# The causal mask of the prompt's window and selected scores, added on TensorE instead of VectorE

## The chip, the cores and the metric

The kernel runs on one core of one Trainium2 chip. The metric is the device time of one execution, in microseconds, of the whole program; lower is better. The times shown are the median of several executions; the profile is one further execution.

## The reference, cut to what matters

One inference step of a two-layer decoder: layer 0 is a causal convolution module, layer 1 is native sparse attention; each has a squared-ReLU MLP and a gated embedding behind it. A prompt of 512 tokens and 64 sample tokens (8 sequences of 8) share the weights. The part that the change touches is the attention of the prompt in layer 1, for its selected-block and its window branch:

```
lw = einsum('bqgrd,bkgd->bqgrk', q_rot, kw) * scale
pw = softmax(where(wmask, lw, NEG), axis=-1)       # wmask: key position <= query position
o_win = einsum('bqgrk,bkgd->bqgrd', pw, vw)
ls, ps, o_sel: the same with the selected branch's keys and values
out = gates0 * o_cmp + gates1 * o_sel + gates2 * o_win
```

With 512 tokens, 16 blocks to choose and 8 there, and a window of 512, both branches see every key up to the query's own position. So a tile of 128 queries needs all key tiles before it in full, and a triangle of the key tile on the diagonal. NEG is -1e30.

## The kernel before, in words

The program is written out by hand for each engine; the engines meet at counted semaphores (`x.then_inc(s, 1)`, `engine.wait_ge(s, n)`). Every engine runs its own instructions strictly in the order written.

Most of the span is dense layers: weights are split into a high and a low part in the type float32r, and three matmuls (lines 611 to 613) with 288 moving columns each make one product. These are the rest of the program, and the change does not touch them.

The prompt's attention is a software-pipelined loop over 64 pairs `PAIRS[i] = (c, r, n)`: chunk c (two heads, 8 of them), query tile n (0 to 3, 128 queries each), branch r (selected or window). A pair has two heads e, which lie on partitions 0 to 63 and 64 to 127. The pair with query tile n has (n+1)*128 keys, so that the work of a pair goes from 1 to 4 units and a chunk has 8 pairs. For each pair:

- TensorE, `p_scores(i)` (lines 944 to 952): two float32 matmuls, one per head, on 64 rows of the array each, into PSUM banks 2*(i%2) and the next. It waits until the exponentials of pair i-2 have been read out of these banks, and signals `p_mm`.
- VectorE, `p_top(i)` (lines 1676 to 1686): adds the 128x128 table `causal` (0 or -1e30) to the diagonal key tile of both heads in PSUM (line 1683), waits for its own write (`chain`), and takes the negated row maximum (line 1685), which signals `p_max`.
- ScalarE, `p_exps(i)` (line 1308): two exponentials with the maximum as bias, which also sum the rows.
- VectorE, `p_sums` (line 1693): reciprocal of the sums. GpSimd (line 586): multiplies the probabilities by the reciprocal and the gate.
- TensorE, `p_transpose(i-3)` (line 961): n+1 transposes for each head. ScalarE (line 1317, head 0) and VectorE (line 1700, head 1) copy them out of PSUM; the transposes of head e wait until the previous pair's copy of e is done.
- TensorE, `p_out(i-4)` (line 978): 2*(n+1) matmuls of 64 weight columns on the two column halves of the array, and line 971 once for a chunk.

In iteration i TensorE issues `p_scores(i)`, `p_transpose(i-3)`, `p_out(i-4)`; VectorE issues `p_top(i)`, `p_sums(i-1)`, `p_move(i-3)`; ScalarE issues `p_move(i-3)`, `p_exps(i)` and, now and then, the copy of a finished chunk (line 1324). Ahead of the loop TensorE waits for `t_fin` (the last sample's heads, VectorE line 1661) and ScalarE for `t_mm` (the transposes of line 901). Behind the loop comes the dense stage "out": ScalarE and VectorE split the attention's result (lines 1032 and 1371), GpSimd splits the weights (line 532) after its last scaling.

`tab("ident")` and `tab("causal")` are 128x128 float32 tables in SBUF. `hb_byte` is the place of a buffer that is free in this stage; its first 16384 bytes per partition hold `pc_t` and `pt_p`.

Of the kernel before, what the change touches and what calls it, by code (L numbers as in the profile page):

```python
# [16 lines left out]
F32R = mybir.dt.float32r  # L17
I32 = mybir.dt.int32
ACT = mybir.ActivationFunctionType
AX = mybir.AxisListType  # L20

P = 128
D = 1024
SEQ = 512
# [160 lines left out]
def program(nc, ext, out):  # L185
    from contextlib import ExitStack
    with ExitStack() as ctx:
        def sb(name, shape, dt=F32):
            return ctx.enter_context(nc.sbuf_tensor(name, shape, dt))

        def sem(name):
            return ctx.enter_context(nc.semaphore(name))
# [3 lines left out]
        def at_byte(name, shape, byte, dt=F32):  # L196
            return nc.alloc_sbuf_tensor_at(name, shape, dt, offset=byte)
# [19 lines left out]
        hb_byte = arena[0]  # L217
# [24 lines left out]
        q_rot = big[:, at:at + C * T].rearrange("p (c t) -> p c t", t=T); at += C * T  # L242
        kv_cmp = big[:, at:at + 4 * T].rearrange("p (c t) -> p c t", t=T); at += 4 * T
        k_rot = big[:, at:at + 4 * T].rearrange("p (c t) -> p c t", t=T); at += 4 * T
# [40 lines left out]
        rec_p = kvc_flat[:, 2160:2168]  # L285
        k_cmp_p = sb("k_cmp_p", [P, 2, 2, NCP])
        w2 = sb("w2", [P, 2, HD])
        c_vec = sb("c_vec", [P, 2])
        gate_s = sb("gate_s", [P, NB, 3])
        pages = sb("pages", [1, NB * PAGES], I32)  # L290
# [3 lines left out]
        ps = ctx.enter_context(nc.psum_tensor("ps", [P, 8, 512], F32))  # L294
# [36 lines left out]
        def tab(name):  # L331
            a, b = CON[name]
            return con[:, a:b]
# [70 lines left out]
        pt_out = [sem("pt_out0"), sem("pt_out1")]  # L404
        po_mm = sem("po_mm")
        ot_out = sem("ot_out")

        block = ctx.enter_context(nc.Block())

# [181 lines left out]
        def _(pe):  # L591
# [96 lines left out]
            for n, (i, m, j) in enumerate(DIAGONALS):  # L688
                t = FIRST["taps"] + i
                first, end = j == TAP_TILES[i][1], j == TAPS - 1  # L690
                if first:
# [4 lines left out]
                                 stop=end).then_inc(tile_done if end else diag_used, 1)  # L696
# [3 lines left out]
            for i, m in enumerate([None] + LATE):  # L700
# [3 lines left out]
                for a in range(2):  # L704
                    last = nc.tensor.matmul(STAT[:, a, :], tab("mean"), src[:, a * HT:(a + 1) * HT],
                                            start=i == 0, stop=i == len(LATE))
# [21 lines left out]
            for a in range(2):  # L728
                for k in range(C):
                    for w, h in ((wg_hi, ha), (wg_lo, ha), (wg_hi, hb)):  # L730
                        last = nc.tensor.matmul(slot(t)[0:48, a, :], w[:, 48 * k:48 * k + 48], chunk(h, k, a * HT, HT),
                                                start=k == 0 and (w, h) == (wg_hi, ha), stop=k == C - 1 and h is hb)
# [3 lines left out]
            for part in range(2):  # L736
# [3 lines left out]
                for i in range(TT):  # L740
# [3 lines left out]
                    for k in range(C):  # L744
                        nc.tensor.matmul(to, chunk(ha, k, i * P, P), wh[:, 256 * k:256 * k + 256], start=k == 0, stop=False)
                        nc.tensor.matmul(to, chunk(ha, k, i * P, P), wl[:, 256 * k:256 * k + 256], start=False, stop=False)
                        last = nc.tensor.matmul(to, chunk(hb, k, i * P, P), wh[:, 256 * k:256 * k + 256], start=False,
                                                stop=k == C - 1)
# [5 lines left out]
            for i in range(TT):  # L754
                rows = P if i < PT else NS
                last = nc.tensor.transpose(ps[0:rows, 2 * (t % 3), 48 * i:48 * i + 48], gates_f[:, i * P:i * P + rows],
                                           tab("ident")[0:48, 0:48])
# [4 lines left out]
            lo, _ = PAR["pe"]  # L762
            for v in range(2):
                for j in range(16):
                    last = nc.tensor.matmul(ps[0:1, 7, P * v:P * (v + 1)], par[:, lo + 16 * v + j:lo + 16 * v + j + 1],
                                            w1[:, v, j, :], start=j == 0, stop=j == 15)
            last.then_inc(c_mm, 1)
            pe.wait_ge(pairs_in, 16 * 4)
            for v in range(2):
                for j in range(16):  # L770
                    last = nc.tensor.matmul(ps[:, 6, 128 * v:128 * v + 124].rearrange("p (g c) -> p g c", g=KV),  # L771
                                            w1[:, v, j, :], kv_pairs[:, v, :, 2 * j:2 * j + 16 * (NCP - 2) + 1:16],
                                            start=j == 0, stop=j == 15)
                last.then_inc(phid_mm, 1)
            pe.wait_ge(c_there, 1)
            for v in range(2):
                last = nc.tensor.transpose(ps[:, 7, 256 + v:257 + v], c_row[:, P * v:P * (v + 1)], tab("ident")[0:1, 0:1])
# [6 lines left out]
            for g in range(2):  # L784
                for k in range(4):
                    last = nc.tensor.matmul(ps[32 * k:32 * k + 32, 7, 64 + 64 * g:128 + 64 * g],
                                            hid_p[:, 1, k % 2, g, :], w2[:, 1, :], start=True, stop=True)
# [24 lines left out]
            for u in range(2 * NB):  # L812
                b, v = u // 2, u % 2
                i = B_OF["cmp_pages", b]
# [3 lines left out]
                for half in range(2):  # L818
                    for j in range(8):
                        rhs = block_at(i, 0, BLK).rearrange("p (a n) -> p a n", a=PAGES)[:, :, 256 * v + 32 * j:256 * v + 32 * j + 32]  # L820
                        last = nc.tensor.matmul(ps[:, 2 * (u % 3) + half, 0:256], w1[:, v, 8 * half + j, :], rhs,  # L821
                                                start=j == 0, stop=j == 7)
# [9 lines left out]
            for b in range(NB):  # L832
                for g in range(2):
                    last = nc.tensor.matmul(ps[64 * g:64 * g + 64, 4, 64 * b:64 * b + 64],
                                            qbd[:, b, g, :, :].rearrange("p e m -> p (e m)"), k_cmp_s[:, b, g, :],
                                            start=True, stop=True)
            last.then_inc(sc_mm, 1)
            for n in range(PT):
                for c in range(C):
                    last = nc.tensor.matmul(ps[:, n, 2 * NCP * c:2 * NCP * (c + 1)], q[:, c, n * P:(n + 1) * P],  # L840
                                            k_cmp_p[:, c // 4, :, :].rearrange("p e c -> p (e c)"), start=True, stop=True)
                last.then_inc(sc_mm, 1)
                if n == 1:
# [5 lines left out]
                    for j in range(4):  # L849
                        last = nc.tensor.transpose(ps[:, 6, 128 * j:128 * j + 128], pc_s[:, 128 * j:128 * j + 128], tab("ident"))  # L850
                    last.then_inc(ct_mm, 1)
            for n in range(PT):
# [5 lines left out]
                for j in range(4):  # L858
                    last = nc.tensor.transpose(ps[:, 4 + n % 2, 128 * j:128 * j + 128], pc[n][:, 128 * j:128 * j + 128],
                                               tab("ident"))  # L860
# [48 lines left out]
            for b in range(NB):  # L909
                if b + 1 < NB:  # L910
                    scores_s(b + 1)
                i = B_OF["sel_pages", b]
# [5 lines left out]
                for k, tiles in enumerate(([0, 128, 256, 384], [512, 640, 768, 896], [1088, 1216, 1344, 1472], [1024, 1600])):  # L918
                    to = t_slot(t_group(b, k))
                    w = P if k < 3 else NS  # L920
                    for j, at in enumerate(tiles):
                        last = nc.tensor.transpose(to[0:w, 128 * j:128 * j + 128], pp[:, at:at + w], tab("ident"))
# [10 lines left out]
                for j in range(4):  # L933
                    nc.tensor.matmul(ps[:, 6, 256:512], pt_s[:, 1024 + 128 * j:1152 + 128 * j],
                                     win[:, 2 + j // 2, 256 * (j % 2):256 * (j % 2) + 256],
                                     start=j == 0, stop=False)
# [7 lines left out]
            def p_scores(i):  # L944
                c, r, n = PAIRS[i]
                if i >= 2:
                    pe.wait_ge(p_exp, i - 1)
                for e in range(2):
                    part = slice(64 * e, 64 * e + 64)
                    last = nc.tensor.matmul(ps[:, 2 * (i % 2) + e, 0:(n + 1) * P], q_rot[part, c, n * P:(n + 1) * P],  # L950
                                            k_rot[part, 2 * r + c // 4, 0:(n + 1) * P], start=True, stop=True)
                last.then_inc(p_mm, 1)

            def p_transpose(i):
# [26 lines left out]
                last.then_inc(po_mm, 1)  # L981

            pe.wait_ge(t_fin, NB)
            N = len(PAIRS)
            for i in range(N + 4):
                if i < N:
# [17 lines left out]
        def _(act):  # L1004
# [140 lines left out]
            for m in range(C):  # L1145
                p = tile("pw1", 2 * m)
# [177 lines left out]
                nc.scalar.activation(attn_t[:, c, 0:SEQ], ps[:, 6 + c % 2, :], ACT.Copy).then_inc(ot_out, 1)  # L1324

            act.wait_ge(t_mm, 5 * NB)
            N = len(PAIRS)
            for i in range(N + 3):
                if i >= 3:
# [21 lines left out]
        def _(dve):  # L1351
# [173 lines left out]
            def chain(ins):  # L1525

                after(step(ins))
# [148 lines left out]
            def p_top(i):  # L1676
                n = PAIRS[i][2]
                dve.wait_ge(p_mm, i + 1)
                if i >= 4:
                    dve.wait_ge(p_exp, i - 3)  # L1680
                lo, col = 2 * (i % 2), 2 * (i % 4)
                s = ps[:, lo:lo + 2, n * P:(n + 1) * P]
                chain(nc.vector.tensor_tensor(s, s, tab("causal").rearrange("p (o k) -> p o k", o=1).to_broadcast((P, 2, P)),
                                              ALU.add))
                nc.vector.tensor_reduce(nmax_p[:, col:col + 2].rearrange("p (e o) -> p e o", o=1), ps[:, lo:lo + 2, 0:(n + 1) * P],
                                        AX.X, ALU.max, negate=True).then_inc(p_max, 1)

# [191 lines left out]
```

## Time and profile before

| what | value |
|---|---|
| median of 3 runs | 1984.52 us (1984.49 to 1991.64) |
| profiled execution, its own time | 1990.01 us |
| its span, first to last instruction | 1987.9 us |
| mean granted TensorE clock | 0.956 of 2.4 GHz |
| TensorE busy | 1836.5 us (92%) |
| VectorE, ScalarE, GpSimd busy | 775.7, 644.1, 601.3 us |
| the loop over the 64 pairs | about 1254.8 to 1411.5 us of the span |

"Busy" is the union of the instructions' durations on an engine; matmuls overlap each other, so the time that a matmul costs in a stream is the distance between starts, not its duration. A float32 matmul shows as two records, a float32r matmul and a transpose as one. "PEclk" is the granted TensorE clock as a share of 2.4 GHz: 1.00 or 0.50, or a mean of both over a stretch.

### The profile page before, as it was taken

Reading aid. Unit: us, or ns where it says so; the run is one execution under the profiler, and the core shown is the slowest. Engines: PE = TensorE matmul, PEld = TensorE weight load, DVE = VectorE, ACT = ScalarE, POOL = GpSimd, SP = SyncE. Lnnn points to the kernel's source line nnn. Section 1 sums busy time; section 2 is a strip of 40 time slices with the busy share of each in tenths; the row PEclk is TensorE's granted clock in tenths of the full one; section 3 lists DMA queues with packets and bytes.
Section 4 is the critical chain, followed back from the end, with each engine's and each line's share of the span. In section 5 each row is a group of like instructions: output and inputs, shape, how many; then the busy total and the mean of one; then the engine's idle time right before and its main releaser. Section 6 shows DMA issues by size and latency. Waiting matters only on the chain.

```text
span 1987.9 us, 30013 instructions
## 1 busy us (share of the span) xinstructions
PE 1836.5 (92%) x12689; PEld 1648.1 (83%) x12689; DVE 775.7 (39%) x1130; ACT 644.1 (32%) x1042; POOL 601.3 (30%) x292
## 2 busy tenths in 40 slices
PE   5999679999999998999899698899878999999998
PEld 5974669999999988999788455466768999999988
DVE  5979535021212245152000633577435121222242
ACT  4243534232222233422111232477433232222231
POOL 3653113333333312332100000355412333333322
PEclk9999779999999999999899799899989999999999
DMA  6253111222222211134542667100111222122211
GB/s 207 85 58 29 43 43 64 85 86 85 85 85 79 79 72 69 64 97 115 165 138 85 222 214 242 43 2 1 55 64 64 85 80 91 65 87 84 85 64 69
DMA packets 62326, 175.86 MB, mean 88 GB/s; under 512 B 22754, under 2 KB 23666, under 8 KB 48690
## 3 DMA queue, kind: packets, MB, share of 16 engines
q1 hardware_dynamic: 59346, 164.66, 26.3%
q0 software_dynamic: 2720, 8.42, 1.2%
q8 instruction: 100, 1.64, 0.3%
q10 hardware_dynamic: 128, 0.88, 0.3%
q14 instruction: 32, 0.26, 0.0%
HBM read 155.55 MB, written 15.41 MB: 86 GB/s over the span
## 4 chain that ended last, share of the span: by engine, by line
PE 83%; DVE 9%; ACT 3%; issue 2%; DMA 1%; SPq 1%; POOL 1%; ACTq 0%; DVEq 0%; POOLq 0%
PE ps L611 20%; PE ps L613 20%; PE ps L612 20%; PE ps L821 6%; PE ps L950 3%; PE ps L961 2%; PE ps L978 2%; DVE ps L1472 2%; PE ps L648 2%; DVE hb L1371 1%; PE ps L931 1%; PE ps L678 1%; PE ps L877 1%; DVE sq_sum L1384 1%; PE ps L771 1%
## 5 line engine op out<-in xcount | busy, mean ns | idle before, releaser
L532 POOL TENSOR_TENSOR w_lo<-w_raw,w_hi 128x2048 fp32r<-128x2048 f32 x98 | 452.9, 4622 | 896.6 <-ACT w_hi L1014 896.6
L611 PE MATMUL ps<-ha,w_hi 128*128 128x288 f32 x1920 | 573.3, 299 | 26.3 <-DVE hb L1371 24.8
L612 PE MATMUL ps<-hb,w_hi 128*128 128x288 f32 x1920 | 571.3, 298 | 0.0
L613 PE MATMUL ps<-ha,w_lo 128*128 128x288 f32 x1920 | 571.1, 297 | 0.0
L611 PEld LDWEIGHTS ps<-ha,w_hi 128*128 128x128 f32 x1920 | 366.0, 191 | 29.9 <-issue 17.6
L612 PEld LDWEIGHTS ps<-hb,w_hi 128*128 128x128 f32 x1920 | 366.1, 191 | 0.0
L613 PEld LDWEIGHTS ps<-ha,w_lo 128*128 128x128 f32 x1920 | 366.0, 191 | 0.0
L611 PE MATMUL ps<-hid_hi,w_hi 128*128 128x288 f32 x1024 | 301.8, 295 | 0.0
L612 PE MATMUL ps<-hid_lo,w_hi 128*128 128x288 f32 x1024 | 301.6, 295 | 0.0
L613 PE MATMUL ps<-hid_hi,w_lo 128*128 128x288 f32 x1024 | 301.6, 295 | 0.0
L1014 ACT ACTIVATE w_hi<-w_raw 128x2048 fp32r<-128x2048 f32 x98 | 186.9, 1907 | 171.4 <-PE ps L613 165.5
L1402 DVE TENSOR_TENSOR sq<-sq 128x576 f32<-128x576 f32 x64 | 94.8, 1482 | 314.1 <-ACT sq L1096 314.1
L613 PEld LDWEIGHTS ps<-hid_hi,w_lo 128*128 128x128 f32 x1024 | 192.3, 188 | 0.0
L612 PEld LDWEIGHTS ps<-hid_lo,w_hi 128*128 128x128 f32 x1024 | 192.1, 188 | 0.0
L611 PEld LDWEIGHTS ps<-hid_hi,w_hi 128*128 128x128 f32 x1024 | 192.0, 188 | 0.0
L1412 DVE TENSOR_TENSOR mix<-ps,mix 128x576 f32<-128x576 f32 x48 | 36.4, 758 | 237.4 <-PE ps L613 237.2
L821 PE MATMUL ps<-ring,w 128*128 128x256 f32 x512 | 115.7, 385 | 0.0
L821 PEld LDWEIGHTS ps<-ring,w 128*128 128x128 f32 x512 | 96.9, 192 | 16.1 <-issue 2.9
L586 POOL TENSOR_SCALAR big<-big,gates 128x128 f32<-128x128 f32 (+3 forms) x128 | 77.0, 611 | 101.5 <-DVE big L1693 100.8
L1472 DVE SCALAR_TENSOR_TENSOR ps<-big,par,ps 128x512 f32<-128x512 f32 x156 | 103.5, 749 | 0.0
L1096 ACT ACTIVATE sq<-ps 128x576 f32<-128x576 f32 x64 | 41.6, 650 | 165.8 <-PE ps L613 165.8
L580 POOL DMA_DIRECT2D out_win<-attn_t x8 | 5.8, 722 | 257.4 <-DMA attn_t<-in_win 257.4
(238 smaller groups left out, 2170.0 us busy)
## 6 DMA issues: line engine op xcount, KB each, us to landing
w_raw<-in_w SPq DMA_DIRECT2D x98, 1024.0 KB, 4.8
ring<-in_cmp_pages SPq DMA_DIRECT2D x64, 256.0 KB, 3.0
ring<-in_sel_pages SPq DMA_DIRECT2D x64, 256.0 KB, 3.2
attn_t<-in_win SPq DMA_DIRECT2D x16, 512.0 KB, 5.4
out_win<-attn_t POOLq DMA_DIRECT2D x8, 1024.0 KB, 5.3
x<-in_x SPq DMA_DIRECT2D x4, 576.0 KB, 5.5
out_y<-x SPq DMA_DIRECT2D x8, 288.0 KB, 2.1
w_raw<-in_ple SPq DMA_DIRECT2D x2, 1024.0 KB, 4.7
```

The source lines that it names most:

```text
L532: nc.gpsimd.tensor_tensor(w_lo[j % 2][:, :], w_raw[:, k, :], w_hi[j % 2][:, :].bitcast(F32), ALU.subtract).then_inc(w_ready, 1)
L586: nc.gpsimd.tensor_scalar(rows, rows, rec_p[:, 2 * (i % 4) + e:2 * (i % 4) + e + 1], gates[:, n, gate:gate + 1], ALU.mult, ALU.mult).then_ ...
L611: nc.tensor.matmul(to, wh, chunk(hi, k, a * HT, HT), start=k == 0, stop=False)
L612: nc.tensor.matmul(to, wh, chunk(lo, k, a * HT, HT), start=False, stop=False)
L613: return nc.tensor.matmul(to, wl, chunk(hi, k, a * HT, HT), start=False, stop=k == C - 1)
L648: last = nc.tensor.matmul(slot(t)[:, a, :], w[:, k, m * P:(m + 1) * P], ple_in[:, k, a * HT:(a + 1) * HT], start=k == 0, stop=k == 1)
L821: last = nc.tensor.matmul(ps[:, 2 * (u % 3) + half, 0:256], w1[:, v, 8 * half + j, :], rhs, start=j == 0, stop=j == 7)
L950: last = nc.tensor.matmul(ps[:, 2 * (i % 2) + e, 0:(n + 1) * P], q_rot[part, c, n * P:(n + 1) * P], k_rot[part, 2 * r + c // 4, 0:(n + 1) ...
L1014: nc.scalar.activation(w_hi[j % 2][:, :], w_raw[:, k, :], ACT.Copy).then_inc(w_hi_ready, 1)
L1096: nc.scalar.activation(halves(raw(name, m)), p, ACT.Relu).then_inc(act_freed, 1)
L1402: nc.vector.tensor_tensor(r, r, r, ALU.mult).then_inc(raw_ready, 1)
L1472: on_way.append(step(nc.vector.scalar_tensor_tensor(to, e, w, sums, ALU.mult, ALU.add)))
```

## The change

TensorE gets, in every pair, two more matmuls behind the two score matmuls: the identity as weights and the causal table as 128 moving columns, both in float32r, accumulated onto the diagonal key tile of each head. VectorE's addition goes, and the wait on its own write with it. The two tables are copied once, by ScalarE, into a float32r buffer `mask_r` behind `pt_p`, ahead of the loop; TensorE waits for both copies before its first pair.

```diff
+        mask_r = at_byte("mask_r", [P, 2, P], hb_byte + 32 * SEQ, F32R)
...
+        mask_ready = sem("mask_ready")
...
                 for e in range(2):
                     part = slice(64 * e, 64 * e + 64)
-                    last = nc.tensor.matmul(ps[:, 2 * (i % 2) + e, 0:(n + 1) * P], q_rot[part, c, n * P:(n + 1) * P],
-                                            k_rot[part, 2 * r + c // 4, 0:(n + 1) * P], start=True, stop=True)
+                    nc.tensor.matmul(ps[:, 2 * (i % 2) + e, 0:(n + 1) * P], q_rot[part, c, n * P:(n + 1) * P],
+                                     k_rot[part, 2 * r + c // 4, 0:(n + 1) * P], start=True, stop=False)
+                for e in range(2):
+                    last = nc.tensor.matmul(ps[:, 2 * (i % 2) + e, n * P:(n + 1) * P], mask_r[:, 0, :], mask_r[:, 1, :],
+                                            start=False, stop=True)
                 last.then_inc(p_mm, 1)
...
             pe.wait_ge(t_fin, NB)
+            pe.wait_ge(mask_ready, 2)
...
             act.wait_ge(t_mm, 5 * NB)
+            nc.scalar.activation(mask_r[:, 0, :], tab("ident"), ACT.Copy).then_inc(mask_ready, 1)
+            nc.scalar.activation(mask_r[:, 1, :], tab("causal"), ACT.Copy).then_inc(mask_ready, 1)
...
                 lo, col = 2 * (i % 2), 2 * (i % 4)
-                s = ps[:, lo:lo + 2, n * P:(n + 1) * P]
-                chain(nc.vector.tensor_tensor(s, s, tab("causal").rearrange("p (o k) -> p o k", o=1).to_broadcast((P, 2, P)),
-                                              ALU.add))
                 nc.vector.tensor_reduce(nmax_p[:, col:col + 2].rearrange("p (e o) -> p e o", o=1), ps[:, lo:lo + 2, 0:(n + 1) * P],
                                         AX.X, ALU.max, negate=True).then_inc(p_max, 1)
```

## Rows read from the trace of the kernel before

**Rows 1.** The profile page: TensorE's busy time, and the chain that ended last.

```profile
PE 1836.5 (92%) x12689; PEld 1648.1 (83%) x12689; DVE 775.7 (39%) x1130; ACT 644.1 (32%) x1042; POOL 601.3 (30%) x292
PE 83%; DVE 9%; ACT 3%; issue 2%; DMA 1%; SPq 1%; POOL 1%; ACTq 0%; DVEq 0%; POOLq 0%
```

**Rows 2.** Busy time by stretch: length, then each engine's busy us (instructions), PEclk.

```profile
1275.00:1402.00 127.00, 125.95 (x1062) 76.64 (x1064) 94.97 (x221) 88.47 (x284) 66.05 (x110) 1.00 0.01 2
1285.49:1303.92 18.43, 18.31 (x156) 11.12 (x155) 13.86 (x33) 12.47 (x42) 9.62 (x16) 1.00 0.01 2
1322.35:1340.93 18.58, 18.35 (x155) 11.12 (x155) 13.90 (x33) 14.05 (x43) 9.62 (x16) 1.00 0.00 1
1254.80:1275.00 20.20, 17.85 (x78) 8.35 (x78) 11.13 (x26) 9.04 (x33) 6.58 (x12) 0.59 0.18 77
```

**Rows 3.** Chain of waits inside one chunk: start us, us, what, xrecords.

```profile
1290.95 1.06 PE ps L950 x4
1292.01 0.81 PE ps L961 x6
1292.82 0.59 PE ps L978 x8
1293.40 0.42 PE ps L950 x4
1293.83 0.48 PE ps L961 x3
1294.31 0.12 issue
1294.42 0.52 PE ps L961 x3
...
1296.17 1.02 PE ps L961 x8
```

**Rows 4.** Groups by line, loop only: line, engine, operation, shapes, count, busy, mean ns.

```profile
L1683 DVE TENSOR_TENSOR ps<-ps,con 128x256 f32<-128x256 f32 x64 | 27.6, 431 | 37.3 <-PE ps L950 36.8
```

**Rows 5.** VectorE in order of time beside the gap at 1294.31: start us, us.

```profile
1292.06 0.43 DVE L1683 TENSOR_TENSOR ps<-ps,con 128x256 f32<-128x256 f32 x1
1292.53 1.23 DVE L1685 TENSOR_REDUCE big<-ps 128x2 f32<-128x1024 f32 x1
1293.74 0.54 DVE L1700 COPY pt_p<-ps 128x384 f32<-128x384 f32 x1
```

**Rows 6.** Chain of waits in two float32r stages: 256 and 288 moving columns.

```profile
908.01 0.12 PE ps L747
1424.34 0.13 PE ps L613
```

**Rows 7.** Weight loads, whole run: float32r, float32, transposes; mean ns behind busy us.

```profile
L612 PEld LDWEIGHTS ps<-hb,w_hi 128*128 128x128 f32 x1920 | 366.1, 191 | 0.0
L931 PEld LDWEIGHTS ps<-ring,sq 128*128 128x128 f32 x128 | 23.7, 190 | 4.4 <-ACT sq L1296 1.0
L961 PEld LDWEIGHTS ps<-con,big 128*128 128x128 f32 x320 | 34.3, 143 | 33.6 <-issue 17.2 <-POOL big L586 14.7
```

**Rows 8.** Float32 matmuls of 64 columns, 128x128 weights: TensorE in order of time.

```profile
1110.77 3.54 PE L840 MATMUL ps<-k_cmp_p,big 128*128 128x64 f32 x29
```

**Rows 9.** Chain of waits ahead of the loop and into its first pair.

```profile
1247.91 0.65 PE ps L931 x3
...
1249.18 1.92 PE ps L934 x8
...
1254.42 0.37 DVE attn_t L1661 x2
...
1254.84 0.82 PE ps L950 x4
...
1255.68 0.45 DVE ps L1683
```

**Rows 10.** ScalarE's copies of an SBUF table of 128x128: duration min/median/max ns.

```profile
L1142 ACT ACTIVATE diag<-con,par x74: 386/401/403, 117.6 to 177.8; 128x128 f32<-128x128 f32 x74
```

**Rows 11.** GpSimd in order of time at the loop's end.

```profile
1404.78 3.13 POOL L586 TENSOR_SCALAR big<-big,gates 128x512 f32<-128x512 f32 x4 [0.93 <-DVE big L1693]
1407.88 9.01 POOL L532 TENSOR_TENSOR w_lo<-w_raw,w_hi 128x2048 fp32r<-128x2048 f32 x2
```

**Rows 12.** Chain of waits from the loop's end into the stage "out".

```profile
1404.68 0.47 DVE pt_p L1700
1405.15 0.14 issue
1405.28 0.52 PE ps L961 x3
...
1412.86 4.66 DVE ha L1371
```

## Prediction

> **What bounds the kernel now.** I read the page's busy line and its chain first: TensorE is busy 92% of the span and holds 83% of the chain [rows 1]. That is an average over stages, so the next view is the busy time by stretch, on the loop that the change touches. From 1275 to 1402 us TensorE is busy 125.95 of 127.00 us at the full clock, VectorE 94.97, ScalarE 88.47, GpSimd 66.05 [rows 2]. A chunk of 8 pairs takes 18.43 us, of which TensorE is busy 18.31 and VectorE 13.86. Busy on TensorE can hide gaps, since the ends of matmuls are modelled. So the third view is the chain of waits inside a chunk, where each piece runs from start to start [rows 3]. The pieces follow each other with nothing between, and their lengths are a plain function of the work: transposes take 0.81 us for 6 and 1.02 us for 8, that is 0.107 us each and 0.16 to 0.17 us for entering and leaving the group. The scores take 1.06 us for 512 columns and 0.42 us for 128, 0.213 us for each 128 columns. A stage that waited on another engine would not keep such lengths. It has one exception in a chunk: 6 transposes that take 0.48 + 0.12 + 0.52 = 1.12 us instead of 0.81, about 0.3 us lost at 1294.31 [rows 3]. What TensorE waits for there is VectorE's copy of head 1, which starts at 1293.74 and takes 0.54 us, behind an addition of 0.43 us and a reduction of 1.23 us [rows 5].
>
> So in steady state the loop is TensorE's, by a margin of a quarter over VectorE, and VectorE costs it about 0.3 us in a chunk. The addition that goes is 64 instructions of 0.431 us, 27.6 us in sum [rows 4], and nearly all of that lies beside TensorE's work.
>
> **What the change removes.** VectorE loses 0.43 us and the hand-over to its own next instruction (0.45 us from start to the next piece in the chain [rows 9]; 0.47 us from start to start [rows 5]) in each pair. Beside TensorE's work this is worth nothing. It is worth something in three places. (a) The gap of about 0.3 us in a chunk: VectorE's copy now comes earlier against TensorE's scores and TensorE arrives later, so the gap closes; 7 chunks from the first such gap behind 1275 make -2.1 us, and shorter gaps in some chunks (18.58 us instead of 18.43 in one, [rows 2]) some -0.2: -2.3 us. (b) The first pairs, where scores, maximum and exponentials hang on each other: part of (d) below. (c) The end: GpSimd scales the last two pairs from 1404.78 for 3.13 us and then splits two weight blocks until 1416.89 [rows 11]; VectorE's 4.66 us part that opens the next stage lies beside that and ends at 1417.52 [rows 12]. The scaling hangs on the reciprocal behind the last pair's reduction. That reduction comes 0.47 us earlier by the missing addition and 0.22 us later by the mask matmuls: -0.25 us. The closed wait of 0.14 us at 1405.15 is inside that.
>
> **What it adds, in each pair.** Two matmuls of 128x128 weights and 128 moving columns. No row of before shows a float32r matmul under 256 columns. Float32r matmuls take 0.12 us from start to start with 256 columns and 0.13 us with 288 [rows 6]: 256 and 288 columns at 2.4 GHz are 0.107 and 0.120 us, so each has some 13 ns on top, and 128 columns would need 0.053 + 0.013 = 0.067 us if nothing else bound them. The weights do: float32 matmuls of 64 columns, whose two records need only 0.053 us of columns each, run at 0.11 to 0.12 us for each record (3.54 us for 29, [rows 8]); and a float32r weight load lasts as long as a float32 one, 191 ns against 190 ns, where that of a transpose lasts 143 ns [rows 7]. So I take 0.11 us for the load of each mask matmul. The two heads' weights are the same, but each matmul carries its own load.
>
> In sequence: the scores leave the 64-row form of the array and the next group enters the 128-row form, before and after the change; before, the transposes pay for that, now the first mask matmul does, with a longer exposed load. Eight float32 matmuls that enter the same way take 1.92 us [rows 9], 0.19 us over 8 steps of 0.216 us (0.65 us for 3), where transposes pay 0.16 to 0.17: the exposed load costs 0.03 to 0.05 us more. Then comes one step of 0.11 us (the second load), and the second mask matmul itself 0.067 us, with the transposes' shorter load under it. First load and step, second matmul: 0.05 + 0.11 + 0.067 = 0.22 to 0.23 us in each pair; I take 0.22. Bounds from rows: 0.13 us if the loads cost nothing (two times 0.067); 0.43 to 0.47 us if 128 columns of float32r take what 128 columns of the float32 scores take, 0.213 us [rows 3]; and 0.37 us if the way from a float32r matmul to a transpose costs an entering and leaving of its own, 0.15 us more.
>
> The Trainium skill speaks to this in "TensorE: Matmul & The Clock Gate", section "LDWEIGHTS": a load takes as many ns as its columns divided by 1.2, 107 ns for 128; the row of 64-column matmuls agrees (0.11 to 0.12 us). The same page, section "Weight-path perf modes", has a rule by which it comes out cheaper: a fast weight load is on when there are 128 weights and the type is not FP32, and float32r might count as such. By the traces a float32r load lasts 191 ns and a float32 load 190 ns, so the trace speaks against it; it is a rival below. "TensorEngine Tiling", section "Key Properties", says that changing the tiling mode drains the engine; the trace shows such a cost at every group (0.16 to 0.19 us), and whether a float32r matmul ahead of a transpose is a change of mode no row shows.
>
> (d) **The first 8 pairs.** This stretch runs at a granted clock of 0.59 in the mean [rows 2], 0.50 in most of it. Pairs 0 to 3 hang on the exponentials; there the score's signal comes later by the masks and an additional change of form (about 0.6 us at half clock) and VectorE saves 0.47: +0.13 us on each of two hops. From pair 4 TensorE binds: two pairs at half clock, 2 x 0.44, and two at full clock, 2 x 0.22. Sum +1.6 us. Bounds 0 and +4.
>
> (e) **Ahead of the loop.** ScalarE's two copies wait for the same transposes as VectorE's line 1661, and TensorE now waits for both. A copy of such a table takes 401 ns [rows 10]; two in a row, overlapped by 0.1 us, end 0.7 us after 1254.42 instead of VectorE's 0.37 us [rows 9]: +0.3 us. Queued behind that wait on TensorE is only the loop itself. The copies read and write SBUF and cover nothing else; ScalarE has nothing to do until the first maximum at 1256.6. Bounds 0.2 and 0.5.
>
> **The sum.** Behind the eighth pair, 55 pairs carry their 0.22 us to the last score: 55 x 0.22 = 12.1. With (a) -2.3, (c) -0.25, (d) +1.6, (e) +0.3: +11.5 us. The rest of the program follows shifted. The profiled execution was 1990.01 us, its span 1987.9; it lies 5.5 us over the median 1984.52, which one of the three runs (1991.64) does too, so such a difference is between executions and I carry the sum over to the median: 1984.5 + 11.5 = 1996.0 us, +0.58%. With 0.19 to 0.26 us for a pair and the bounds of (d) and (e) this case runs from 1992 to 2001.
>
> **The rivals.**
> 1. Four passes: float32r with only 128 columns costs what float32 costs. For it: all float32r rows have 256 columns or more, so nothing shows that the low price holds below. Against: at 256 and 288 the time is columns over the clock plus a constant. A pair pays 0.47 us, 0.25 more: 57 x 0.25 = +14: 2010 us.
> 2. A change of form between mask and transposes: +0.15 us a pair, 57 x 0.15 = +8.5: 2004.5 us. The change from 64 to 128 rows shows the price; between two 128-row forms no row shows it.
> 3. Cheap masks, on the other side (not slower): the weight loads of float32r are fast or lie under the drain of the scores. A pair pays 0.13 us: 55 x 0.13 = 7.2, (d) halves to 0.8, the rest as above: +5.7, 1990.2 us, within what can be told from no change. It turns into a gain at a price for a pair under about 0.04 us, which no row comes near. The rule on fast loads named above would be its mechanism.
> 4. VectorE sets the loop after all, and TensorE's gapless look is the model's. Then 64 x 0.47 = 30 us would go and some 1970 us be left. Against it: VectorE's 75% of the stretch, and group lengths that follow the work alone.
>
> **How the numbers follow.** Forecast 0.55, rival 1 0.2, rival 2 0.1, rival 3 0.12, rival 4 0.03. Times of this kernel can be told from no change at about 0.5%, 9.9 us. The forecast's own range straddles that a little (1994.4), and so do single executions 7 us apart: three quarters of it count as slower. Slower: 0.41 + 0.2 + 0.08 = 0.69; faster: rival 4, 0.03; the rest, 0.28, within 0.5%. The range takes in rival 3 and rival 1: 1989.5 to 2011.
>
> **What would show it.** Right: the added matmuls start about 0.16 and then 0.11 us apart, and the transposes less than 0.1 us behind the second; a chunk takes 18.4 + 8 x 0.22 - 0.3 = 19.9 us instead of 18.43; the piece of three and three transposes has no gap; VectorE's busy time in the loop falls by 27.6 us while TensorE stays over 98%. Wrong: steps of 0.2 us or two records for a mask matmul (rival 1); 0.15 us or more between the second mask and the transposes (rival 2); a chunk at or under 18.4 us (rival 4); new waits on `p_exp` or `p_scaled` on TensorE, which I cost at nothing, because every pair gives the other engines more time than before.

## The result, and the profile after

| | median of runs | lowest to highest | profiled execution | its span | its granted clock |
|---|---|---|---|---|---|
| before | 1986.94 us (5 runs) | 1984.49 to 1991.64 | 1990.01 us | 1987.9 us | 0.956 |
| after | 2002.59 us (5 runs) | 1997.77 to 2006.75 | 1997.77 us | 1995.8 us | 0.96 |

The ratio after/before is 1.0074, 95% interval 1.0055 to 1.0092: the change makes the kernel slower by 0.55 to 0.92%, 11 to 18 us. I had forecast 1996.0 us with a range of 1989.5 to 2011 and a chance of 0.69 for slower. The kernel before came out at 1986.94 us here, and at 1988.5 to 1989.3 us in three comparisons with 23 to 29 runs each below. My base of 1984.5 us rested on three runs and was low by 2 to 5 us.

The profile page of the kernel after, its busy line: TensorE has 11.6 us more and 128 records more, VectorE 27.2 us and 64 instructions less than in [rows 1].

```profile
PE 1848.1 (93%) x12817; PEld 1664.0 (83%) x12817; DVE 748.5 (38%) x1066; ACT 644.8 (32%) x1044; POOL 600.8 (30%) x292
```

Busy time by stretch of the kernel after, columns as in [rows 2]: the stretch of the loop and one chunk in it.

```profile
1275.00:1402.00 127.00, 127.00 (x1080) 82.59 (x1077) 66.84 (x153) 81.61 (x260) 59.70 (x101) 1.00 0.01 2
1280.32:1300.39 20.07, 20.07 (x172) 13.09 (x171) 10.58 (x25) 12.44 (x42) 9.57 (x16) 1.00 0.01 2
```

A chunk takes 20.07 us where it took 18.43 [rows 2], and in it TensorE has no idle time at all, while VectorE's busy time falls from 13.86 to 10.58 us. A chunk's length is read from the chain of waits, as the distance between two starts of the piece of 1.05 us that comes once in a chunk (line 971 before, line 976 after).

The chain of waits inside that chunk, kernel after, beside [rows 3]. Its lines 952, 955, 966 and 983 are the scores, the mask matmuls, the transposes and `p_out`:

```profile
1286.27 1.06 PE ps L952 x4
1287.33 0.37 PE ps L955 x2
1287.70 0.68 PE ps L966 x6
1288.38 0.59 PE ps L983 x8
1288.97 0.42 PE ps L952 x4
1289.39 0.37 PE ps L955 x2
1289.76 0.68 PE ps L966 x6
...
1292.04 0.90 PE ps L966 x8
```

Three things can be read here. The scores take what they took (1.06 and 0.42 us). The two mask matmuls (L955) are a piece of 0.37 us, and the transposes behind them are shorter by 0.12 to 0.13 us (0.68 for 6 against 0.81, 0.90 for 8 against 1.02), because the mask now pays for entering the group: 0.37 - 0.125 = 0.245 us a pair, net. And the six transposes that broke into 0.48 + 0.12 + 0.52 us in [rows 3] are one piece.

### The profile page after: what moved, and what is told of

It is laid out like the page before. It is cut to its first block, busy times and chain, and to the rows that moved or that the text cites. A ratio compares the mean times of both kernels' runs of the same rounds, so it can differ in the third digit from the quotient of the medians.

```text
span 1995.8 us, 30207 instructions
## 1 busy us (share of the span) xinstructions
PE 1848.1 (93%) x12817; PEld 1664.0 (83%) x12817; DVE 748.5 (38%) x1066; ACT 644.8 (32%) x1044; POOL 600.8 (30%) x292
## 4 chain that ended last, share of the span: by engine, by line
PE 84%; DVE 8%; ACT 3%; issue 1%; DMA 1%; POOL 1%; SPq 1%; ACTq 0%; DVEq 0%; POOLq 0%
PE ps L613 20%; PE ps L615 20%; PE ps L614 20%; PE ps L823 6%; PE ps L952 2%; PE ps L983 2%; DVE ps L1480 2%; PE ps L966 2%; PE ps L650 2%; PE ps L933 1%; PE ps L955 1%; DVE hb L1379 1%; PE ps L680 1%; PE ps L879 1%; DVE sq_sum L1392 1%
## 5 line engine op out<-in xcount | busy, mean ns | idle before, releaser
L613 PE MATMUL ps<-ha,w_hi 128*128 128x288 f32 x1920 | 573.2, 299 | 24.9 <-DVE hb L1379 23.9
```

What stands on the lines that cost most here:

```text
L613: nc.tensor.matmul(to, wh, chunk(hi, k, a * HT, HT), start=k == 0, stop=False)
```

## The experiments

Of each run the ratio to the kernel before, measured beside it, is given, and the length of a steady chunk, in which the clock is full. In the kernels with mask matmuls and in no_mask the steady chunks repeat to 0.01 us, far finer than the times; in the kernel before, four of six take 18.43 us and two 18.58. (chunk - 18.12) / 8 is the price of a pair's mask, where 18.12 us is the chunk without any mask (no_mask). Line numbers in the lines shown are those of each run's own kernel, and shift by one or two.

**before_again: how fine is the comparison?** No edit.

> The kernel before, unchanged, as a second profile. Its steady chunk (8 pairs) must again take 18.43 us. Open is the first chunk: it took 20.1 us before, with 17.1 us at the half clock, and 17.1 us in the changed kernel, with 6.8 us at the half clock. If the shorter stretch at the half clock is chance (it falls differently from one execution to the next), this run may show a first chunk unlike 20.1 us, or the changed kernel's later profiles will show other values than 17.1. If the change itself shortens it (more work on TensorE), this run shows 20 us again and every kernel with mask matmuls about 17.

1.0014, interval 1.0001 to 1.0028; chunk 18.43 us. The first chunk, from the first score of pair 0 to that of pair 8, takes 18.96 us where it took 20.08, with 13.7 us at half clock instead of 17.1: it differs between executions of one program. The same kernel against itself reads 0.14% off, with an interval that leaves out 1, so nothing under 0.3% is read from a ratio here; the chunks must carry it.

**no_mask: the floor.** The mask is left out.

```diff
-                s = ps[:, lo:lo + 2, n * P:(n + 1) * P]
-                chain(nc.vector.tensor_tensor(s, s, tab("causal")...to_broadcast((P, 2, P)), ALU.add))
```

> The kernel before with the addition of the mask left out altogether (neither engine adds it; the outputs of the prompt are then not causal). Theory (TensorE sets the loop, VectorE costs it one gap of 0.3 us in a chunk): a steady chunk takes 18.15 us instead of 18.43, the total is some 3 us under before, which timing alone can hardly tell. Rival (VectorE's in-order chain sets the loop and TensorE only looks gapless): 8 x 0.47 = 3.8 us less in a chunk, 30 us less in all.

0.9983, 0.9969 to 0.9997. Two starts of the once-a-chunk piece:

```profile
1302.97 1.05 PE ps L971 x2
1321.09 1.05 PE ps L971 x2
```

18.12 us a chunk: taking 64 x 0.43 us from VectorE is worth 0.31 us a chunk. From the first score to the first matmul of the next stage, this trace is 3.9 us shorter than before_again's, which also has 13.7 us at half clock at the loop's start: 0.2% of the time, within the ratio's interval of 0.03 to 0.31%. This is about all that the change could ever have won. Rival 4 (VectorE sets the loop, -1.5%) falls.

**both: VectorE's addition kept beside the mask matmuls.**

```diff
+                s = ps[:, lo:lo + 2, n * P:(n + 1) * P]
+                chain(nc.vector.tensor_tensor(s, s, tab("causal")...to_broadcast((P, 2, P)), ALU.add))
```

> The mask matmuls of the changed kernel with VectorE's addition kept beside them (the mask is added twice). Theory: TensorE pays 0.245 us a pair whether VectorE is relieved or not; a steady chunk takes 18.15 + 8 x 0.245 = 20.1 us plus whatever VectorE's addition still costs it, 0 to 0.3 us: 20.1 to 20.4. Total as the changed kernel, at most 3 us more. Rival (the relief of VectorE is worth much and offsets a larger cost of the masks): a chunk of 22 us or more.

1.0078, 1.0061 to 1.0095. Once-a-chunk starts, and the one group of transposes in a chunk that is longer than 0.68 us:

```profile
1291.95 1.05 PE ps L976 x2
...
1301.39 0.86 PE ps L966 x6
...
1312.21 1.05 PE ps L976 x2
```

20.25 to 20.26 us, 0.18 more than with the masks alone: the addition costs TensorE 0.18 us a chunk even here. So the slowdown is the matmuls' own (18.43 to 20.25 with VectorE's work as it was), and VectorE's relief gives little of it back.

**four_masks: each mask matmul twice.**

```diff
-                for e in range(2):
+                for k in range(4):
+                    e = k // 2
...
-                                            start=False, stop=True)
+                                            start=False, stop=k % 2 == 1)
```

> Each head's mask matmul is issued twice (the mask is added twice), so four in a pair. Theory (a mask matmul costs its weight load, about 0.11 us, whatever waits there are): a chunk takes 20.07 + 16 x 0.11 = 21.8 us and the total is 64 x 0.22 = 14 us over the changed kernel. Rival (most of the cost is paid once, for the change of form or a later signal to VectorE, and the masks themselves are 0.067 us each): 20.07 + 16 x 0.067 = 21.1 us, +8.6 us in all.

1.0159, 1.014 to 1.0178. The masks' piece, and two once-a-chunk starts:

```profile
1295.29 1.05 PE ps L977 x2
...
1302.74 0.59 PE ps L956 x4
...
1317.14 1.05 PE ps L977 x2
```

21.85 us, 1.78 more than after for 16 more matmuls: 0.111 us each.

**one_mask: the mask of head 1 left out.**

```diff
-                                     ..., start=True, stop=False)
-                for e in range(2):
+                                     ..., start=True, stop=e == 1)
+                for e in range(1):
```

> As the changed kernel with the mask matmul of head 0 alone (head 1 of each chunk is left without its mask). It parts the price of a pair, 0.245 us, into the first and the second mask matmul. By four masks in a pair each further one costs 0.111 us: a chunk of 20.07 - 8 x 0.111 = 19.2 us and 0.134 us for the first. If the first pays for the change of form alone and the rest is free (rival), 19.9 to 20.0 us.

1.0013, 0.9998 to 1.0028. The mask's piece, and the once-a-chunk starts:

```profile
1300.66 0.26 PE ps L955
1301.17 1.05 PE ps L976 x2
...
1320.34 1.05 PE ps L976 x2
```

19.17 us: the first mask costs (19.17 - 18.12) / 8 = 0.131 us and the second (20.07 - 19.17) / 8 = 0.112 us, the same as the third and fourth. Each mask is a step of 0.11 us, and the first has 0.02 us on top.

**half_cols: 64 moving columns instead of 128.** The mask is left out of the first 64 keys of the diagonal tile.

```diff
-                    last = nc.tensor.matmul(ps[:, 2 * (i % 2) + e, n * P:(n + 1) * P], mask_r[:, 0, :], mask_r[:, 1, :],
+                    last = nc.tensor.matmul(ps[:, 2 * (i % 2) + e, n * P + 64:(n + 1) * P], mask_r[:, 0, :], mask_r[:, 1, 64:P],
```

> As the changed kernel, but each mask matmul has 64 moving columns instead of 128 (the mask is left out of the first 64 keys of the diagonal tile). It asks what the 0.111 us of a float32r mask matmul is: the load of 128 weight columns, or 128 moving columns. Theory (the load): a chunk stays at 20.0 to 20.07 us. Rival (the columns, at 0.067 us for 128 or twice that): 16 x 0.027 to 16 x 0.053 us less, 19.2 to 19.65 us.

1.007, 1.0041 to 1.0098. Two once-a-chunk starts, and the load of the masks in the loop's stretch:

```profile
1309.54 1.05 PE ps L976 x2
1329.61 1.05 PE ps L976 x2
```

```profile
L955 PEld LDWEIGHTS ps<-mask_r 128*128 128x128 f32 x102 | 15.2, 188 | 22.1 <-issue 20.4
```

20.07 us, as with all 128 columns, so the columns don't set the price. The loads' records stay too: 188 ns in the mean here, and 188 ns with all columns in the same stretch of the kernel after.

**mask_bf16: the mask's two tables in bfloat16.**

```diff
-        mask_r = at_byte("mask_r", [P, 2, P], hb_byte + 32 * SEQ, F32R)
+        mask_r = at_byte("mask_r", [P, 2, P], hb_byte + 32 * SEQ, BF16)
```

> As the changed kernel, with the identity and the causal table copied to bfloat16 instead of float32r (1, 0 are exact in it, and a rounded -1e30 masks as well). Columns are read once in both. Theory (a mask matmul costs its weight load): if a bfloat16 load of 128 columns lasts as long as float32r's 0.11 us, nothing changes, 20.07 us a chunk; if it is fast (a quarter to a half), the pair pays 0.10 to 0.15 us instead of 0.245: 19.0 to 19.3 us a chunk and 6 to 9 us less in all, still over the kernel before. Rival (the price is the 128 columns and the change between matmul and transpose, not the load): within 0.02 us a pair, that is 19.9 to 20.1 us.

0.9997, 0.9979 to 1.0014. The weight loads of the mask after, and of bfloat16 (count, busy us, mean ns):

```profile
L955 PEld LDWEIGHTS ps<-mask_r 128*128 128x128 f32 x128 | 19.6, 193 | 29.4 <-issue 27.5
```

```profile
L956 PEld LDWEIGHTS ps<-mask_r 128*128 128x128 bf16 x128 | 7.3, 98 | 29.3 <-issue 27.3
```

Its chain: the masks' piece and the transposes behind it, then two once-a-chunk starts.

```profile
1296.87 1.05 PE ps L977 x2
...
1303.53 0.22 PE ps L956 x2
1303.75 0.66 PE ps L967 x6
...
1315.57 1.05 PE ps L977 x2
```

18.71 us: 0.074 us a pair instead of 0.245, with the same two matmuls of 128 columns. The records of the load halve (193 to 98 ns), and the piece falls from 0.37 to 0.22 us.

The starts of the single instructions say where the time goes. Distances from start to start in us, medians over the pairs behind the first nine that have at least two transposes a head (single pairs lie within 0.005 us of them, but for one of 0.136 in the kernel before):

| run | 1st to 2nd mask | last mask to 1st transpose | 1st to 2nd transpose | sum |
|---|---|---|---|---|
| before | | | 0.165 | 0.165 |
| after | 0.164 | 0.112 | 0.136 | 0.412 |
| one_mask | | 0.167 | 0.132 | 0.299 |
| half_cols | 0.132 | 0.112 | 0.166 | 0.410 |
| mask_bf16 | 0.066 | 0.056 | 0.116 | 0.238 |

Later transposes follow each other by 0.109 us in all of them. With 64 columns the second mask starts 0.032 us earlier, but the second transpose does not: that time comes back one step later. In bfloat16 the step is 0.056 us, about what 128 columns need at 2.4 GHz (0.053 us, an estimate), and the pair's net price of 0.074 us is under two such steps, since the transposes no longer pay for entering. So the float32r price isn't set by its columns, and it goes with the type of the tables. That it is the weight load is the reading that fits best: the load's record halves with the step. The kernel before has a sign of it in float32, whose matmuls of 64 columns take 0.11 us a record with 128 weight columns [rows 8]. With 64 weight columns, two side by side on the array's column halves, 32 records start within 1.0 us: 0.03 us each, 0.06 us for one half (`--source L834` of its trace):

```profile
L834 PE MATMUL ps<-big x32: 222/222/270, 1099.6 to 1100.6; 128*64 128x64 f32 x32
```

Not tested is a float32r mask with fewer weight columns; a fixed least time of a float32r matmul, whatever it loads, is not excluded.

**mask_f32: the tables themselves, in float32.**

```diff
-                    last = nc.tensor.matmul(ps[:, 2 * (i % 2) + e, n * P:(n + 1) * P], mask_r[:, 0, :], mask_r[:, 1, :],
+                    last = nc.tensor.matmul(ps[:, 2 * (i % 2) + e, n * P:(n + 1) * P], tab("ident"), tab("causal"),
```

> As the changed kernel, with the mask matmuls in plain float32, read from the tables themselves. This is the first rival of the prediction: two records for each matmul, 0.213 us by its columns. The pair pays 0.05 + 2 x 0.213 = 0.48 us: 18.12 + 8 x 0.48 = 22.0 us a chunk, 15 us over the changed kernel in all. If float32r had been no cheaper than float32 at 128 columns it would equal the changed kernel's 20.07 us.

1.0127, 1.0103 to 1.0151. Masks' piece and once-a-chunk starts:

```profile
1303.33 0.64 PE ps L955 x4
1306.92 1.05 PE ps L976 x2
...
1328.96 1.05 PE ps L976 x2
```

22.04 us and two records for a matmul: 0.49 us a pair. This is the price of rival 1, and float32r with 128 columns pays half of it.

**after_again: the size of the whole, again.** No edit.

> The changed kernel, unchanged, as a second profile. The steady chunk must take 20.07 us again. The first chunk took 17.1 us in its first profile with 6.8 us at the half clock, but 23.4 us with 20.5 at the half clock when VectorE's addition was kept beside the masks. If the clock there is chance, this run gives another value than 17.1, between 17 and 25; if the change itself shortens the stretch at half clock, 17.1 again.

1.0063, 1.0041 to 1.0085; chunk 20.07 us, median 2001.12 us. It agrees with the first comparison (1.0055 to 1.0092).

**bf16_early: bfloat16, and ScalarE's copies of the tables moved ahead of the sample loop.**

```diff
+            nc.scalar.activation(mask_r[:, 0, :], tab("ident"), ACT.Copy).then_inc(mask_ready, 1)
+            nc.scalar.activation(mask_r[:, 1, :], tab("causal"), ACT.Copy).then_inc(mask_ready, 1)
             window_out(0)
...
-            nc.scalar.activation(mask_r[:, 0, :], tab("ident"), ACT.Copy).then_inc(mask_ready, 1)
-            nc.scalar.activation(mask_r[:, 1, :], tab("causal"), ACT.Copy).then_inc(mask_ready, 1)
             N = len(PAIRS)
```

> As the bfloat16 masks, with ScalarE's two copies of the tables moved ahead of the sample's attention loop, some 120 us earlier. Chunk 18.71 us as before. Theory: TensorE's first score comes 0.37 us or so behind the last sample transposes again and not 0.7, so 0.3 us less; the total stays level with the kernel before, 1.5 us over the version without gaps. Rival (the copies cost nothing, TensorE waits for VectorE there anyway): no change of that distance.

0.9997, 0.9981 to 1.0012; chunk 18.71. The chain ahead of the loop, kernel after and then this one:

```profile
1250.67 0.42 PE ps L903 x2
...
1251.11 0.31 ACT mask_r L1333
1251.42 0.21 ACT mask_r L1334
...
1251.77 0.49 PE ps L952 x4
```

```profile
1253.66 0.42 PE ps L904 x2
...
1254.11 0.36 DVE attn_t L1670 x2
...
1254.52 0.49 PE ps L953 x4
```

1.10 us from the transposes to the first score with the copies in between, 0.86 without: (e) is confirmed in place and size (0.3 forecast, 0.24 measured), and it is far too small to show in the times.

**act_copy4: can the gap at VectorE's copy be had more cheaply?** The kernel before, with head 1's copy of `pt_p` on ScalarE in one pair of eight.

```diff
+                if i % PER_C == 4:
+                    act.wait_ge(pt_mm[1], i + 1)
+                    nc.scalar.activation(pt_p[:, i % 2, 1, ...], ps[:, 5, ...], ACT.Copy).then_inc(pt_out[1], 1)
...
             def p_move(i):
                 n = PAIRS[i][2]
+                if i % PER_C == 4:
+                    return
```

> The kernel before (VectorE adds the mask), but in one pair of eight, the one whose copy of head 1 left TensorE waiting 0.3 us, ScalarE copies both heads. Theory (that copy is all that VectorE costs TensorE): the gap goes and a chunk takes 18.12 to 18.2 us instead of 18.43 to 18.58, as with no mask at all; in total 2 to 3 us under the kernel before, hardly more than timing can tell. Rival (the wait moves to ScalarE, whose exponentials come 0.5 us later in that pair and hold up the scores two pairs on): 18.4 us or more.

0.9994, 0.9977 to 1.001. The unbroken piece that was split in [rows 3], and two once-a-chunk starts:

```profile
1300.51 1.05 PE ps L971 x2
...
1308.84 0.81 PE ps L961 x6
...
1318.63 1.05 PE ps L971 x2
```

The chunk is 18.12 us, the floor of no_mask, without touching the mask: in such a chunk the gap was head 1's copy alone. One chunk takes 18.28 us, and the two in which ScalarE splits a weight block take 18.57, where they took 18.58 before. The gain behind the first chunk is some 1.4 us and can't be told from none in the times.

**act_copy4_late: the same, and the splits moved from pairs 32 and 40 to 37 and 45.**

```diff
-                if i in (32, 40):
+                if i in (37, 45):
...
-                    split_weight(W_OF["out"] + (i - 32) // 8)
+                    split_weight(W_OF["out"] + (i - 37) // 8)
```

> As the kernel before with ScalarE taking head 1's copy in one pair of eight, and with ScalarE's two weight splits of this loop (1.9 us each) moved from iterations 32 and 40 to 37 and 45. With the splits where they were, five chunks took 18.12 to 18.28 us and the two with a split 18.57. Theory (in those two the split delays the exponentials of the small pairs right behind it): every steady chunk takes 18.12 to 18.25 us, 2.5 to 3 us under the kernel before in all. Rival (the split costs 0.4 us wherever it stands, for ScalarE has no slack beside the extra copy): those two chunks stay at 18.5 or more.

1.0000, 0.9984 to 1.0016; a miss. The two chunks grow to 19.36 and 19.35 us. Two once-a-chunk starts, and between them the chain where TensorE waits:

```profile
1338.60 1.05 PE ps L971 x2
...
1344.10 0.59 ACT w_hi L1014
1344.69 1.09 issue
...
1357.96 1.05 PE ps L971 x2
```

ScalarE in order of time in the same place:

```profile
1343.98 1.91 ACT L1014 ACTIVATE w_hi<-w_raw 128x2048 fp32r<-128x2048 f32 x1
1345.78 0.39 ACT L1317 ACTIVATE pt_p<-ps 128x256 f32<-128x256 f32 x1
```

The split of 1.91 us stands ahead of head 0's copy, which ends 1.1 to 1.2 us late. The chain calls 1.09 us of it "issue", since it ascribes a wait to what came last; the timeline names the engine. ScalarE is busy only 70% of the loop in the kernel before [rows 2], and yet a piece of 1.9 us at this place costs TensorE 1.2 us, where at the old place it cost 0.45 (18.57 against 18.12). A busy share says nothing of the length of the holes.

## Why the prediction was right

- **What bounds the loop.** Right. TensorE was busy 125.95 of 127.00 us and is now busy all of it; taking VectorE's additions off gives 0.31 us a chunk and no more.
- **(a), the gap.** Right: its 0.3 us a chunk are gone, by no_mask at 18.12 us and by act_copy4 for the reason given, head 1's copy behind addition and reduction. For the seven chunks behind the first, no_mask is 2.45 us shorter than the kernel before, with 2.3 forecast.
- **The price of a pair.** The mechanism held (two steps of 0.11 us, an entry moved from the transposes to the mask), with the weight load as its likely but not wholly shown cause, and the size was a little low: 0.245 us for 0.22. The term that was mis-sized is "the second mask matmul itself 0.067 us, with the transposes' shorter load under it". In order of start, the second mask follows the first by 0.164 us and the first transpose follows the second mask by 0.112 us, where I had less than 0.1. The second mask costs a whole step of 0.112 us (one_mask, four_masks) and not its columns. The longer exposed load of the first was put at 0.03 to 0.05 us and 0.02 is there, but not where I had it: entering takes a mask no longer than a transpose (0.164 against 0.165 us), and it is the second transpose that comes late, by 0.136 us instead of 0.109. Why is open. So the chunk is 20.07 us instead of the forecast 19.9.
- **(d), the first pairs.** The first chunk of after_again takes 21.58 us against 20.08 before, each with 17.1 us at half clock: +1.5 us, with 1.6 forecast. Before, 0.4 us of those 17.1 lie ahead of the first score, which makes some 0.2 us of the 1.5 (an estimate). The masks' piece takes 0.62 us at half clock, with about 0.6 forecast.
- **(e), ahead of the loop.** +0.24 us (1.10 against 0.86 us from transposes to first score), with 0.3 forecast.
- **(c), the end.** -0.10 us (15.27 against 15.37 us from the start of the last record of the last scores to the next stage's first matmul), with -0.25 forecast. The mis-sized term is "0.22 us later by the mask matmuls". The chain of waits there, kernel before and then kernel after:

```profile
1401.81 1.08 PE ps L950 x4
...
1402.92 0.44 DVE ps L1683
...
1403.39 0.04 DVE big L1685
```

```profile
1406.71 1.06 PE ps L952 x4
1407.77 0.38 PE ps L955 x2
...
1408.17 0.04 DVE big L1690
```

The reduction comes 1.58 us behind the start of the scores' piece before and 1.46 us after, 0.12 us earlier and not 0.25. The wait of 0.14 us behind VectorE's copy, which I took for closed, is still there. VectorE waits for the whole piece of the masks, 0.38 us. The 0.125 us in it that the transposes save elsewhere is saved behind VectorE's signal and so doesn't count here. The other runs agree: the stretch is 14.92 us in no_mask, 15.10 in mask_bf16, 15.15 in one_mask and 15.52 in mask_f32, each 14.92 us and the length of its masks' piece (0.22, 0.26, 0.64 us) within 0.04 us.

- **The sum by the traces.** Seven chunks behind the first: six steady ones 9.6 us longer, the last one 1.4 (17.92 against 16.52 from its first score to its last score record), 11.0 in all, for which the prediction had 12.1 - 2.3 = 9.8. With +1.5, +0.24 and -0.10: +12.6 us, 0.63%, with +11.5 forecast. Both timed intervals hold it (0.55 to 0.92% and 0.41 to 0.85%). That the medians differ by 15.6 us in the first comparison and by 11.8 in the second lies within the spread between executions. Of the 6.6 us by which the first median lies over the forecast, 2.4 are the low base and 1.1 the low sum.
- **The rivals.** 1 (four passes): float32 costs 0.49 us a pair, float32r half. 2 (a change of form between mask and transposes): the step is 0.112 us, as between a second and a third mask (four_masks), and only the second transpose comes 0.027 us late, far from 0.15. 3 (cheap masks): refuted for float32r, at 0.245 us a pair with loads of 193 ns; true for bfloat16, at 0.074 us a pair. 4: refuted by no_mask.

Of the Trainium skill's rules, the one in "TensorE: Matmul & The Clock Gate", section "Weight-path perf modes" (a fast weight load with 128 weights of a type that is not FP32) fits bfloat16 here, 98 ns for a load, and float32r stands with FP32: 193 ns. By the same page's section "LDWEIGHTS", 128 columns over 1.2 give 107 ns, and the measured step of a mask is 0.111 to 0.112 us.

**The profiled executions alone** would have misled: they are 7.8 us apart, not 12.6. The rest is in the loop's first chunk, which begins at half the clock: 17.06 us against 20.08, 3.0 us less where 1.5 more were due. (Ahead of the loop the execution after is 3.1 us ahead and behind it 3.1 us longer; these two cancel.) The first 20 us of the loop, in one execution of the kernel before and two of the kernel after (PEclk is the third number from the end):

```profile
1254.84:1274.84 20.00, 17.68 (x76) 8.25 (x76) 10.97 (x26) 9.04 (x33) 6.58 (x12) 0.58 0.18 77
```

```profile
1251.77:1271.77 20.00, 19.84 (x122) 11.65 (x123) 9.62 (x23) 11.91 (x42) 9.16 (x16) 0.83 0.17 70
```

```profile
1255.39:1275.39 20.00, 19.99 (x77) 10.02 (x77) 6.82 (x17) 8.24 (x31) 5.89 (x12) 0.57 0.16 68
```

The granted clock is 0.58 before, and 0.83 and 0.57 in two executions of the program after. The stretch at 1.2 GHz (half) lasts 17.1 us before and 13.7 in before_again, 6.8 and 17.1 us in the two after. The first chunk of the kernel after is 17.06 us in the one execution and 21.58 in the other. What decides how long it stays low is open.

**The best version.** None beats the kernel before by what the times can tell. mask_bf16 beats the changed kernel by 13 us (0.9997 against 1.0063 in the same comparison; 10.7 us from the first score to the next stage, by two traces with 6.8 us at half clock each) and ties with the kernel before in the times; its chunk is 0.28 us longer. act_copy4 has the shortest steady chunks that keep the mask. Even with no mask at all only 0.2% would be won.

## What to carry to other kernels

Work may be moved off an engine only for what that engine costs the path: here 27.6 us of VectorE's time were worth 0.31 us a chunk and 3.9 us in all, which leaving the work out shows in one run. The float32r matmul with few moving columns did not cost its columns but 0.11 us, with 64 as with 128, most likely its weight load, so adding a table by TensorE is cheap only in bfloat16 (0.074 us for two), where the values allow that. What is put ahead of a signal delays all that waits for it, also where the sum on its own engine is smaller: 0.38 us at the loop's end for 0.245 a pair. Where executions of one program differ by more than the change, take the steady stage's period from the trace, multiply, and check the edges at equal clock.

## What the runs showed of the hardware

- Two bfloat16 mask matmuls cost a pair 0.074 us, two in float32r 0.245, two in float32 0.49, with 128x128 weights and 128 columns. Loads last 98, 193 and, for float32 elsewhere in the run, 190 ns in the records. A bfloat16 matmul may be added onto scores in PSUM that float32 matmuls have written, with no cost that shows.
- With float32r, 64 moving columns take as long as 128 (chunk 20.07 us in both).
- The first two starts of a group of 128 columns behind the scores are 0.164 to 0.165 us apart, float32r masks or transposes alike, where later ones are 0.109 to 0.112 apart; with the mask ahead of them, six transposes take 0.68 us instead of 0.81.
- Float32 transposes of 128x128 follow each other by 0.109 us at full clock.
- The length of the stretch at half clock at the loop's start varied from 6.8 to 23.9 us over the executions of these kernels, and twofold and more between two executions of one program.
